# Output stage of a hybrid attention layer: the turn of gated y, on TensorE and ScalarE or by transfers of the SP queue

## The reference

```
y = concat([y_a * silu(a_g), y_b * silu(b_g)], axis=-1)   # (2048, 1024)
h = h + einsum('bsm,md->bsd', y, w_out)                    # w_out (1024, 1024)
```

## Time and profile before

| | us |
|---|---|
| median of three runs | 1729.15 (1726.45 to 1731.18) |
| the profiled execution | 1727.61 |
| its span | 1725.8 |
| output stage in the span | about 1517 to 1725.8 |

### The profile page before, as it was taken

One profiled execution on the slowest core, in us unless ns is written; L12 is line 12 of the kernel. 1 busy time (PEld: TensorE's weight loads), 2 busy tenths in 40 slices (PEclk: granted clock), 3 DMA queues, 4 the chain that ended last, 5 costly groups with the idle time before them and its releaser, 6 DMA issues. The chain is left out here.

```text
span 1725.8 us, 39450 instructions
## 1 busy us (share of the span) xinstructions
PE 1603.3 (93%) x14224; PEld 941.7 (55%) x14224; DVE 1187.9 (69%) x1650; ACT 1130.3 (65%) x1458; POOL 563.8 (33%) x474
## 2 busy tenths in 40 slices
PE   6899999999997199999999999999999999959998
PEld 3455555555554046556655665566556665634444
DVE  6555455445445488899889988998889888643232
ACT  8454454454454078888888888888888888843332
POOL 0000000000000056566656665666666565700000
PEclk9999999999998589999999999999999999979999
DMA  8112212212212933223322332323332332145553
GB/s 302 59 56 82 68 53 83 68 48 88 68 33 63 195 117 78 61 60 89 76 60 68 82 76 65 81 66 87 73 69 57 92 76 61 39 142 167 184 179 113
DMA packets 245025, 154.72 MB, mean 90 GB/s; under 512 B 63857, under 2 KB 228209, under 8 KB 244977
## 3 DMA queue, kind: packets, MB, share of 16 engines
q1 hardware_dynamic: 244976, 154.10, 33.6%
HBM read 111.95 MB, written 41.97 MB: 89 GB/s over the span
## 5 line engine op out<-in xcount | busy, mean ns | idle before, releaser
L870 POOL TENSOR_TENSOR p_pl<-p_p,p_ph 128x512 f16<-128x512 f32 x384 | 505.4, 1321 | 900.2 <-ACT p_ph L906 840.3
L921 DVE TENSOR_REDUCE p_part<-p_mx 128x2 f32<-128x1024 f32 x384 | 468.3, 1219 | 91.9 <-PE p_mx L999 73.1
L897 ACT ACTIVATE p_p<-p_st 128x1024 f32<-128x1024 f32 x384 | 392.1, 1021 | 137.3 <-PE p_st L1030 83.3
L535 PE MATMUL p_ring<-p_w_hi,p_xT 128*128 128x512 f16 (+3 forms) x1536 | 391.7, 341 | 9.9 <-DVE p_w_lo L419 6.9
L906 ACT ACTIVATE p_ph<-p_p 128x1024 f16<-128x1024 f32 x336 | 355.1, 1057 | 18.3
L949 DVE TENSOR_TENSOR p_pl<-p_p,p_ph 128x512 f16<-128x512 f32 x384 | 330.2, 860 | 9.5 <-ACT p_ph L906 8.7
L535 PE MATMUL p_ring<-p_w_lo,p_xT 128*128 128x512 f16 (+3 forms) x768 | 261.7, 341 | 0.0
L535 PEld LDWEIGHTS p_ring<-p_w_hi,p_xT 128*128 128x128 f16 x1536 | 151.8, 99 | 132.5 <-issue 13.7
L1062 PE MATMUL p_acc<-p_vas,p_ph 128*128 128x129 f16 x2048 | 207.8, 221 | 0.0
L1063 PE MATMUL p_acc<-p_vas,p_pl 128*128 128x65 f16 x2048 | 201.0, 193 | 0.0
L1062 PEld LDWEIGHTS p_acc<-p_vas,p_ph 128*128 128x128 f16 x2048 | 180.6, 97 | 36.1 <-issue 14.3
(11 more groups left out here) (135 smaller groups left out, 2261.5 us busy)
## 6 DMA issues: line engine op xcount, KB each, us to landing
p_vbs<-scratch_vb SPq DMA_DIRECT2D x16, 1028.0 KB, 6.3
p_xin<-in_x SPq DMA_DIRECT2D x16, 512.0 KB, 3.7
scratch_g<-p_g SPq DMA_DIRECT2D x16, 512.0 KB, 3.5
p_kb<-scratch_kb SPq DMA_DIRECT2D x32, 256.0 KB, 5.3
p_gt<-scratch_g SPq DMA_DIRECT2D x16, 512.0 KB, 4.8
p_xr<-in_x SPq DMA_DIRECT2D x16, 512.0 KB, 4.3
out<-p_res SPq DMA_DIRECT2D x16, 512.0 KB, 3.0
p_w_raw<-in_w_in SPq DMA_DIRECT2D x6, 1024.0 KB, 7.2
```

The costliest lines, as they stand in the source:

```text
L535: last = pe.matmul(ring[n % 3][:, 0:w], a, b, start=(k == 0 and m == 0), stop=(k == len(steps) - 1 and m == len(terms) - 1))
L870: pool.tensor_tensor(pl[:, s % NP, 1, :], p32[:, s % N32, QB:], ph[:, s % NP, 1, :], ALU.subtract).then_inc(s_lop, 1)
L897: act.activation(p32[:, s % N32, :], st[:, s % 2, :, :].rearrange("p a b -> p (a b)"), ACT.Exp, scale=scale).then_inc(s_exp, 1)
L921: dve.tensor_reduce(part[:, e // MPAIRS % 3, 2 * c:2 * c + 2], mx[:, :, :], AX, ALU.max).then_inc(s_red, 1)
```

## The change

The two halves of gated y are turned by two transposing DMAs per tile on the SP queue, straight from `yh` and `yl` to `yT`. TensorE's transposes, ScalarE's copies, the identity and the PSUM buffers `tp` go. SP's `tile(t)` begins with the turn of tile t+1, ahead of the loads of tile t+2; SP's loop over tiles is written out instead of a loop with a register. ScalarE waits for the hi transfer before it writes `yh` again, VectorE for the lo transfer before `yl`, TensorE for both before its products.

```diff
-        eye = sb("eye", [P, P], F16)
-        tp = [ps(f"tp{s}", [P, KT, P], F16) for s in range(2)]
...
+            def turn(t, h, free):
+
+                sp.wait_ge(s_yh, t + 1)
+                if free:
+                    sp.wait_ge(s_po, t * 2 - 2)
+                sp.dma_start_transpose(yT[:, h, 0], yh[:, :]).then_inc(s_yt, 16)
+                sp.wait_ge(s_yl, t + 1)
+                sp.dma_start_transpose(yT[:, h, 1], yl[:, :]).then_inc(s_ytl, 16)
+
+            turn(0, 0, False)
+
             def tile(t, h, i, first, last):
+                if not (last and h == 1):
+                    turn(t + 1, 1 - h, not (first and h == 0))
                 if not last:
 
                     sp.wait_ge(s_yg, t * 2 + 2)
...
-            loop(sp, tile)
+            for t in range(TILES):
+                tile(t, t % 2, t // 2, t < 2, t >= TILES - 2)
...
-        @block.gpsimd
-        def _(pool):
-            pool.memset(eye[:, :], 0.0).then_inc(s_eye, 1)
...
                 if not (first and h == 0):
-                    act.wait_ge(s_tp, t * 2)
+                    act.wait_ge(s_yt, t * 16)
                 act.activation(yh[:, :], yg[:, h, :], ACT.Copy).then_inc(s_yh, 1)
...
-                for s in range(2):
-                    act.wait_ge(s_tp, t * 2 + s + 1)
-                    if not first:
-
-                        act.wait_ge(s_po, t * 2 - 2)
-                    act.activation(yT[:, h, s], tp[s][:, :, :], ACT.Copy).then_inc(s_yt, 1)
...
                 if not (first and h == 0):
-                    dve.wait_ge(s_tp, t * 2)
+                    dve.wait_ge(s_ytl, t * 16)
                 dve.tensor_tensor(yl[:, :], yg[:, h, :], yh[:, :], ALU.subtract).then_inc(s_yl, 1)
...
             def tile(t, h, i, first, last):
-                pe.wait_ge(s_yt, t * 2 + 2)
+                pe.wait_ge(s_yt, t * 16 + 16)
+                pe.wait_ge(s_ytl, t * 16 + 16)
...
-                    if c == 0 and not (last and h == 1):
-                        turn(t + 1, False)
```

More of the change, by code:

```diff
@@ L1119, in phase3 @@
         s_wlo = sem("w_lo")
-        s_eye = sem("eye_ready")
         s_y = [sem("y_loaded0"), sem("y_loaded1")]
@@ L1127, in phase3 @@
         s_yl = sem("y_lo")
-        s_tp = sem("yT_in_psum")
-        s_yt = sem("yT_in_sbuf")
+        s_yt = sem("yT_hi_turned")
+        s_ytl = sem("yT_lo_turned")
         s_po = sem("out_in_psum")
@@ L1170, in tile @@
                     sp.dma_start(xr[:, h, :], xt[t + 2]).then_inc(s_x[h], 16)
-            loop(sp, tile)
+            for t in range(TILES):
+                tile(t, t % 2, t // 2, t < 2, t >= TILES - 2)
             for h in range(2):
                 sp.wait_ge(s_out[h], PAIRS * 16)
-        @block.gpsimd
-        def _(pool):
-            pool.memset(eye[:, :], 0.0).then_inc(s_eye, 1)
-            pool.wait_ge(s_eye, 1)
-            pool.affine_select(out=eye[:, :], in_=eye[:, :], compare_op=ALU.not_equal, fill=1.0,
-                               base=0, pattern=[[-1, P]], channel_multiplier=1).then_inc(s_eye, 1)
         @block.scalar
@@ L1291, in tile @@
                     mm.then_inc(s_po, 1)
-                    if c == 0 and not (last and h == 1):
-                        turn(t + 1, False)
-            pe.wait_ge(s_eye, 2)
-            turn(0, True)
             loop(pe, tile)
```

## The result

| | before | after |
|---|---|---|
| median, us | 1729.2 | 1771.7 (1769.69 to 1773.86) |
| profiled span, us | 1725.8 | 1768.7 |

The ratio is 1.0241, 95% interval [1.0227, 1.0255]: 42.5 us slower. The forecast was slower too, but by 239 us. The time is close to that of the rival with 256-byte runs, which gave 1766 us.

What follows compares the result with a forecast made beforehand. The prediction took a closed loop through the loads, not TensorE, to bound the output stage. 1725.8 + 208 for 13 periods + 20 at the start + 10.8 at the end + 3.3 outside the span gave 1968 us, range 1745 to 2215.

Steps and rivals of the forecast that it cites:

- the rival with 256-byte runs: Output stage's DMA queue: each turning transfer moves in 1024 runs of 256 bytes, 1.5 us each; 1766 us, chance 0.20.
- The loop that bounds the stage: Output stage: residual, store, loads, silu, gate and next residual form a closed loop of 11.82 us; TensorE isn't in it.
- TensorE's and ScalarE's savings: Output stage: 0.89 us of transposes and two 1012 ns copies removed per tile aren't waited for, so they gain nothing.
- The turn stands in the loop, ahead of the loads: SP queue: two 256 KB transfers per tile precede the loads of tile t+2, making the period 11.82 us plus both transfers.
- The size of X: Time of one turning transfer in the DMA queue: taken as 8.0 us, from 8192 runs of 32 bytes.
- The Trainium skill's two rules: Turning transfer's price: 1309 ns per 128 x 128 block gives about 2047 us; regular DMA speed, 350 to 400 GB/s, some 1743.
- The waits on SP cost nothing, and what is left is the time in the queue: SP's waits around the turn: under 0.5 us, hidden by 1 MB of DMA; only the transfers' queue time counts.
- Start and end: Outside the 13 periods: the first tile's residual ends 20 us later, and the part after the last period grows 10.8 us.
- Not slower: Output stage: transfers run in the DMA's idle gap of 5 us a period, loads overtaking them; 1724 us, chance 0.07.

Runs made afterwards that it cites:

- the shifted kernel before: The kernel before the change, with SP loading y and gate one tile further ahead and SP's loop over tiles written out: 1721.53 us, ratio 0.9950.

## Why the prediction was wrong

- *The loop that bounds the stage, and a TensorE busy for 96% of it as no bound.* Right. It was the part on which the sign rested, and the shifted kernel before shows it: an earlier issue of the loads, with SP's loop written out, took 0.57 us off each period and nothing off TensorE's work.
- *TensorE's and ScalarE's savings are worth nothing here.* Right as long as the loop stands.
- *The turn stands in the loop, ahead of the loads.* Right, and shown by putting it behind them: 1727.13 us.
- *The size of X.* **The step that failed**: "I take 8.0 us", 8192 pieces of 32 bytes. The transfer goes in 256-byte packets, 1056 of them, and takes 1.28 us of the engines; two lengthen the period by 3.27 us, 1.63 each. It lands 4.2 us after its issue in the median, not 8 and more. The price per packet from the earlier trace rows was a quarter too high (24.0 ns against 19.3), and with 1024 packets it gave 1.5 us. That this comes so near 1.63 is in part luck: the packets alone would have given less, and the issue of a turn had no price. What was wrong was the choice of the piece, which no row supported: "one side can't go in long runs" was an argument, not a measurement, and the geometric mean of two ends that differ by 200 is no evidence either. With X = 1.63 the sum would have been 13 x 3.26 = +42.4 for the periods.
- *The Trainium skill's two rules.* The Trainium skill's 1309 ns of "VectorE: DVE Perf Modes" (The three transpose paths), taken eight times, isn't what this trace shows: a transfer of eight blocks takes 1.28 us of engine time, about as long as the Trainium skill gives for one block, and 3.2 us at the least from issue to landing. The Trainium skill's rule in "Advanced Engine Details and Errata" (X-Bar Transpose (TRN2)) is nearer. But 256 KB in 1.28 us is 205 GB/s, under the 350 to 400 it states, and a copy of the same bytes cost half as much in the period (0.84 against 1.63 us).
- *The waits on SP cost nothing, and what is left is the time in the queue.* Half right. I gave the issue of a turn no price of its own, though I had counted each DMA's issue in the loop. It is 1.27 us with free engines, three times a plain DMA's. In the changed kernel it is about as long as the transfer, so it adds little: a turn's 1.63 in the period is 0.35 us above its 1.28 on the engines, and how much of that is the issue stays open. In the kernel with each turn cut in two it sets the period.
- *Start and end.* +20 and +10.8 were worked out with X = 8. Measured +2.8 and -2.4. For 256-byte runs I had +1 and -4.1; the difference at the end is mostly the clock: tile 15's 48 products took 11.9 us instead of 10.37, after an idle stretch from 1750.25 to 1753.02, in which the granted clock fell from 1.00 to 0.50. That TensorE runs at the 1.2 GHz level after such stretches was foreseen; that it did so after idle stretches of only 4.6 us (in the period) and 2.8 us (here) was not.
- *Rivals.* The one with 256-byte runs, at a chance of 0.20, had the packets, the period (14.9 us against 15.09) and the time within 6 us; it was named and priced, and not chosen. "Not slower" fell: the loads do stay behind the turn. Its idea of using the DMA's idle gap is what the kernel with loads further ahead does, by moving the loads instead.

## What to carry to other kernels

Read the chain for a closed loop before the busy shares: an engine busy for 96% of the stage was not the bound, and the DMA whose issue closed the loop decided what an insertion on the SP queue costs. A transposing transfer was cheap here where the loop waited for nothing behind it in its queue, so put the loads that close a loop ahead of it, or prefetch one tile further, and only then count what the other engines are spared. Where an operation has no row, the choice of its unit is the forecast: state each unit's result, and give a geometric middle no more weight than its neighbours.

## What the runs showed of the hardware

- A transposing DMA of float16 within SBUF, 128 x 1024: 1056 packets, 262 KB, 1.28 us on 16 engines (205 GB/s), 3.2 us from issue to landing at the least, where the plain copy of the same size took 2.2 at the least and 144 packets.
- Its issue on SP: 1.27 us for 128 x 512, 1.23 to 1.27 for 128 x 1024, 1.92 at the least for 128 x 2048; with full DMA engines 1.7 to 2.5 us for 128 x 1024, up to 3.4 in the kernels with the loads first or further ahead.
- Plain DMAs on SP beside turning ones on ScalarE's queue: the issue of yb grew from 0.51 to 0.93 us, the rate sank to 106 to 179 GB/s for 3 us at a share near 1, and a turn took 1.81 us of the 16 engines.
